# State-space mixer: softplus and products between input units, bounded differences on ScalarE, output tiles inside the head loop and the norm

## What is computed

```python
def pool_ssd_mixer(h, w_in, pool_w, pool_scale, conv_w, conv_b, dt_bias, a_log, d_skip, norm_g, w_out):
    proj = h @ w_in
    u_pool, z, xbc, dt_raw = jnp.split(proj, [...], axis=-1)
    y_pool = multiscale_pool(u_pool, pool_w, pool_scale)
    xbc = jax.nn.silu(causal_depthwise_conv(xbc, conv_w, conv_b))
    xs, bm, cm = jnp.split(xbc, [...], axis=-1)
    dt = jax.nn.softplus(dt_raw + dt_bias)
    a = -jnp.exp(a_log)
    y = ssd_chunked(xh, dt, a, bm, cm)           # two chunks of 128 tokens, 16 heads of 64, 2 groups, state 128
    y = (y + d_skip * xh).reshape(...) * jax.nn.silu(z)
    y = group_rmsnorm(y) * norm_g                # two groups of 512
    return jnp.concatenate([y_pool, y], axis=-1) @ w_out
```

## Time and profile before

| | us |
|---|---|
| median of three runs | 2388.79 |
| lowest, highest of them | 2385.91, 2414.0 |
| the profiled execution, its own time | 2413.47 |
| its span in the profile | 2411.6 |

### The profile page before, as it was taken

The page is one execution under the profiler, slowest core; times in us unless marked ns, Lnnn a source line. Parts: engine busy times, 40 slices in busy tenths (PEclk is TensorE's granted clock), DMA queues, the critical chain, the costliest instruction groups (busy, mean ns, idle before and its releaser), DMA issues.

```text
span 2411.6 us, 46117 instructions
## 1 busy us (share of the span) xinstructions
PE 2282.1 (95%) x18404; PEld 2192.5 (91%) x18404; DVE 1414.0 (59%) x2021; ACT 1166.9 (48%) x1559; POOL 496.2 (21%) x250
## 2 busy tenths in 40 slices
PE   8989999988999899998999999998999999789998
PEld 7869799987999899996899999996899999778998
DVE  4554289955689859685468653365633434356544
ACT  5411166546556544464344454455544443545654
POOL 0013000010000135421035434410044400000343
PEclk9869699999999899996899999998999999889999
DMA  6200167843388568752268845542355455513552
GB/s 247 101 4 1 36 249 301 314 160 122 132 322 298 193 244 331 277 214 96 75 228 349 297 175 191 187 169 105 129 195 195 147 191 195 149 70 123 192 176 103
DMA packets 62224, 439.06 MB, mean 182 GB/s; under 512 B 7228, under 2 KB 7612, under 8 KB 9638
## 3 DMA queue, kind: packets, MB, share of 16 engines
q1 hardware_dynamic: 59472, 430.75, 48.5%
q0 software_dynamic: 976, 2.63, 0.7%
q10 hardware_dynamic: 1670, 4.17, 0.5%
HBM read 434.89 MB, written 2.62 MB: 181 GB/s over the span
## 4 chain that ended last, share of the span: by engine, by line
PE 77%; DVE 10%; issue 6%; ACT 5%; DMA 2%; DVEq 1%; POOL 0%; SPq 0%; ACTq 0%; POOLq 0%
PE ps L276 19%; PE ps L278 19%; PE ps L277 19%; DVE mix L580 3%; PE ps L290 2%; PE ps L298 2%; PE ps L292 2%; PE ps L404 1%; ACT w_hi L255 1%; DVE w_lo L261 1%; PE ps L393 1%; DVE acc L688 1%; DMA ring<-in_weights 1%; DVE acc L682 1%; PE ps L953 1%
## 5 line engine op out<-in xcount | busy, mean ns | idle before, releaser
L276 PE MATMUL ps<-h_hi,w_hi 128*128 128x256 f32 x3512 | 985.1, 280 | 9.4 <-DVE h_lo L2180 4.9
L277 PE MATMUL ps<-h_lo,w_hi 128*128 128x256 f32 x3512 | 982.1, 280 | 0.0
L278 PE MATMUL ps<-h_hi,w_lo 128*128 128x256 f32 x3512 | 981.7, 280 | 0.0
L261 DVE TENSOR_TENSOR w_lo<-ring,w_hi 128x2048 fp32r<-128x2048 f32 x273 | 626.0, 2294 | 566.0 <-ACT w_hi L255 561.6
L255 ACT ACTIVATE w_hi<-ring 128x2048 fp32r<-128x2048 f32 x335 | 640.6, 1913 | 186.8 <-PE ps L278 175.3
L276 PEld LDWEIGHTS ps<-h_hi,w_hi 128*128 128x128 f32 x3512 | 665.6, 190 | 13.1 <-DVE h_lo L2180 5.1
L277 PEld LDWEIGHTS ps<-h_lo,w_hi 128*128 128x128 f32 x3512 | 668.8, 190 | 0.1
L278 PEld LDWEIGHTS ps<-h_hi,w_lo 128*128 128x128 f32 x3512 | 664.5, 189 | 0.0
L276 PE MATMUL ps<-g_hi,w_hi 128*128 (+1 forms) x1232 | 346.8, 282 | 12.5 <-DVE g_lo L710 12.0
L277 PE MATMUL ps<-g_lo,w_hi 128*128 (+1 forms) x1232 | 345.4, 280 | 0.0
L278 PE MATMUL ps<-g_hi,w_lo 128*128 (+1 forms) x1232 | 345.3, 280 | 0.0
(11 more groups left out here) (395 smaller groups left out, 2588.7 us busy)
## 6 DMA issues: line engine op xcount, KB each, us to landing
ring<-in_weights SPq DMA_DIRECT2D x335, 1024.0 KB, 4.8
mix<-in_modw SPq DMA_DIRECT2D x72, 1024.0 KB, 5.0
mix<-in_c_ssd ACTq DMA_DIRECT2D x1, 1536.0 KB, 8.1
bias_rows<-mix POOLq DMA_DIRECT2D x1, 1536.0 KB, 36.0
x<-in_x SPq DMA_DIRECT2D x1, 1024.0 KB, 4.9
mix<-in_c SPq DMA_DIRECT2D x2, 512.0 KB, 5.8
mix<-bias_rows POOLq DMA_DIRECT2D x1, 1024.0 KB, 8.2
out_xT<-hf SPq DMA_DIRECT2D x1, 1024.0 KB, 4.3
```

Of the source, the lines that this page charges most:

```text
L261: dve.tensor_tensor(w_lo[:, n % SLOTS], ring[:, n % SLOTS], w_hi[:, n % SLOTS], ALU.subtract).then_inc(lo_ready[n % SLOTS], 1)
L276: pe.matmul(o, w[0], a_hi, start=first, stop=False, **kw)
L277: pe.matmul(o, w[0], a_lo, start=False, stop=False, **kw)
L278: return pe.matmul(o, w[1], a_hi, start=False, stop=last, **kw)
```

## The change

The order of the weight columns becomes B and C, x, dt (padded to 128), u, z; so dt is in the seventh unit and the last half unit holds the end of z. The loop is written out for 13 units, and what used to stand after it is put between units: C B^T and the transposed B ahead of unit 6, the transposes of x and of dt and dt*a ahead of unit 10, the sums ahead of unit 11, the rows ahead of unit 12. The softplus runs in turn 7 and 8; ScalarE takes Silu of z straight from PSUM. The bounded difference moves from VectorE (`min(row - a_cs, 0)`) to ScalarE (`Relu(a_cs - row)`, and Exp of its negative). The y products alternate between the two heads. `warm` matmuls stand in the pair loop, and `fill` puts tiles of the first two ab_out units in the loop and in the norm. The squares of the first three quarters move from ScalarE to GpSimd, which also adds them in part. `hi` and `lo` of one unit, ab_in + 15 (the third unit of ab_out), are no longer issued in the loop: `hi` stands after the pair loop, `lo` behind the last `low`.

```diff
@@ pool
-            pool.wait_ge(z_free, zbase["ab_in"] + 8)
+            pool.wait_ge(z_free, zbase["ab_in"] + 9)
...
+            for j in range(3):
+                s = slice(2 * j, 2 * j + 2)
+                pool.wait_ge(*after(f"dve:ssd.yz{j}"))
+                pool.tensor_tensor(hf[:, s], sd_y[:, s], sd_y[:, s], ALU.mult).then_inc(*step(f"pool:ssd.gsq{j}"))
...
+        SD_Y_BANK = (5, 6, 7, 6)
+        SD_FILL = {5: 3, 6: 3, 7: 3, 8: 3}
@@ pe
-            a_stage_pe(pe, "ab_in", "ssd", 13, half_last=True)
+            for l in range(count["ab_in"]):
+                n = BASE["ab_in"] + l
+                if l == 6:
...
+                if l == 10:
+
+                    pe.wait_ge(*after("act:ssd.silu5"))
+                    pe.wait_ge(*after("dve:ssd.cbT"))
+                    pe.wait_ge(*after("act:ssd.btok"))
...
+                    pe.wait_ge(*after("dve:ssd.adt"))
...
+            def outer(p):
+                for e in range(2):
+                    done = pe.matmul(bank((p + 1) % 2, 2, T)[:, e], sd_sel[0:16, 2 * p + e],
+                                     sd_row[0:16].rearrange("p c t -> p (c t)"), start=True, stop=True)
+                done.then_inc(*step(f"pe:ssd.a{p}"))
...
+            queue = [(l, kk, b) for l in range(2) for kk in range(2) for b in range(8)]
...
+                    if kk == 0 and b == 0:
+                        pe.wait_ge(lo_ready[s], u // SLOTS + 1)
+                        if l == 0:
+                            pe.wait_ge(*after("dve:ssd.plo"))
+                            pe.wait_ge(*after("dve:ssd.y0"))
...
+            pe.wait_ge(*after("act:ssd.row"))
+            outer(0)
             pe.wait_ge(z_free, zbase["ab_in"] + 13)
...
+            outer(1)
+            pe.wait_ge(*after("dve:ssd.xdt"))
+            warm(3)
             pe.wait_ge(*after("dve:ssd.xdec"))
...
+            warm(2)
+            for p in range(1, 9):
+                if 2 <= p < 8:
+
+                    pe.wait_ge(*after(f"act:ssd.ea{p - 2}"))
+                    outer(p)
+                if p == 2:
...
+                if p < 5:
+                    warm(1)
+                else:
+                    fill(SD_FILL[p])
                 q = p - 1
...
+                pe.wait_ge(*after(f"dve:ssd.g{q}"))
+                o = [ps[SD_Y_BANK[q // 2]][64 * e:64 * e + 64, T * (q % 2):T * (q % 2) + T] for e in range(2)]
+                for e in range(2):
+                    pe.matmul(o[e][:, 0:P], sd_xdt[:, 0, 2 * q + e], sd_dm[q % 2][:, e, 0], start=True, stop=True)
...
+            fill(5)
+            pe.wait_ge(*after("pool:ssd.gs0"))
...
+            fill(2)
+            pe.wait_ge(*after("act:ssd.gsq3"))
...
+            fill(4)
             pe.wait_ge(*after("dve:ssd.rs"))
...
-            b_stage_pe(pe, "ab_out", ["dve:ssd.plo", None, "dve:ssd.ylo0", "dve:ssd.ylo1", "dve:ssd.ylo2", "dve:ssd.ylo3"], "ssd")
+            fill(len(queue))
+            for l in range(2, 6):
+                pe.wait_ge(*after(f"dve:ssd.ylo{l - 2}"))
@@ act
+            for p in range(8):
+                act.wait_ge(*after(f"pe:ssd.a{p}"))
+                if p >= 2:
+                    act.wait_ge(*after(f"pe:ssd.y{p - 2}"))
+                for e in range(2):
+                    for c in range(NCH):
+                        done = act.activation(sd_dm[p % 2][:, e, c], bank((p + 1) % 2, 2, NCH, P)[:, e, c], ACT.Relu, scale=-1.0,
+                                              bias=sd_acs[:, c, 2 * p + e:2 * p + e + 1])
+                done.then_inc(*step(f"act:ssd.m{p}"))
+                act.activation(sd_ce[p % 2], bank((p + 1) % 2, 2, NCH, P)[:, :, 1], ACT.Exp).then_inc(*step(f"act:ssd.ea{p}"))
+                act.wait_ge(*after(f"act:ssd.m{p}"))
+                act.activation(sd_dm[p % 2], sd_dm[p % 2], ACT.Exp, scale=-1.0).then_inc(*step(f"act:ssd.e{p}"))
...
+                if p == 3:
+
+                    act.wait_ge(*after("pe:ssd.pool"))
...
+            hi(act, BASE["ab_in"] + 12 + SLOTS)
@@ dve
+                if l < 12:
+                    lo(dve, BASE["ab_in"] + l + SLOTS)
...
+                if p == 4:
+                    dve.wait_ge(*after("act:ssd.phi"))
+                    for g in range(4):
+                        done = dve.scalar_tensor_tensor(out=h_lo[:, g], in0=bank(2 + g // 2, 2, T)[:, g % 2],
...
+            gated(0)
+            for j in range(1, 4):
+                gated(j)
+                low(j - 1)
+            low(3)
+            lo(dve, BASE["ab_in"] + 12 + SLOTS)
             b_stage_dve(dve, "ab_out", owed=2)
```

More of the change, by code:

```diff
@@ L1735, in ssd_pe @@
             pe.wait_ge(*after("dve:ssd.xdec"))
-            pe.wait_ge(*after("act:ssd.btok"))
-            pe.wait_ge(*after("act:ssd.dend"))
-            pe.wait_ge(*after("act:ssd.row"))
             for g in range(2):
@@ L1768, in ssd_pe @@
-            pe.wait_ge(*after("pool:ssd.d"))
-            for g in range(4):
-                done = pe.matmul(bank(6 + g // 2, 2, T)[:, g % 2], sd_pw[:, g], sd_pd[:, g], start=True, stop=True)
-            done.then_inc(*step("pe:ssd.pool"))
-            for j in range(4):
-                pe.wait_ge(*after(f"act:ssd.gsq{j}"))
-                for c in range(NCH):
-                    for b in (2 * j, 2 * j + 1):
-                        g = b // 4
-                        done = pe.matmul(ps[1][:, 2 * c + g:2 * c + g + 1], hf[:, b, c * P:(c + 1) * P], ones[:, 0:1],
-                                         start=b == 0 and c == 0, stop=b == 7 and c == 1, skip_group_check=True)
+                done.then_inc(*step(f"pe:ssd.prev{g}"))
@@ new lines, in ssd_pe @@
+            sums = ps[1]
+            fill(5)
+            pe.wait_ge(*after("pool:ssd.gs0"))
+            for c in range(NCH):
+                for b in range(2):
+                    pe.matmul(sums[:, 2 * c:2 * c + 1], hf[:, b, c * P:(c + 1) * P], ones[:, 0:1],
+                              start=b == 0 and c == 0, stop=b == 1 and c == 1, skip_group_check=True)
+            pe.wait_ge(*after("pool:ssd.gs1"))
+            for c in range(NCH):
+                pe.matmul(sums[:, 2 * c + 1:2 * c + 2], hf[:, 4, c * P:(c + 1) * P], ones[:, 0:1], start=False, stop=False,
+                          skip_group_check=True)
@@ L1780, in ssd_pe @@
+            fill(2)
+            pe.wait_ge(*after("act:ssd.gsq3"))
+            for c in range(NCH):
+                for b in (6, 7):
+                    done = pe.matmul(sums[:, 2 * c + 1:2 * c + 2], hf[:, b, c * P:(c + 1) * P], ones[:, 0:1],
+                                     start=False, stop=b == 7 and c == 1, skip_group_check=True)
             done.then_inc(*step("pe:ssd.gss"))
+            fill(4)
             pe.wait_ge(*after("dve:ssd.rs"))
@@ L1891, in ssd_dve @@
+            dve.wait_ge(*after("dve:ssd.xdt0"))
             dve.wait_ge(*after("act:ssd.dend"))
@@ L1923, in ssd_dve @@
[L1923 to L1928 removed]
+                    dve.wait_ge(*after("pool:ssd.d"))
+                    for r in (q - 1, q):
+                        done = dve.scalar_tensor_tensor(out=sd_y[:, r], in0=sd_cb[:, r], scalar=V("ssd_d_2", r),
+                                                        in1=bank(SD_Y_BANK[q // 2], 2, T)[:, r % 2], op0=ALU.mult, op1=ALU.add)
```

305 lines of the change are left out of this document (160 added, 145 removed).

## The result

The changed kernel takes 2382.94 us (median of 20 runs, 2359.61 to 2404.44) against 2395.69 of the kernel before measured with it (20 runs, 2385.91 to 2414.0). The ratio on record is 0.9913, 95% interval [0.9889, 0.9937]: 15 to 27 us less, and inside the 2% band. The quotient of the two medians is 0.9947, 12.8 us less, which lies outside that interval; so the gain in the whole time is known only roughly, and the stages of the profiles say more. The forecast was 2369.3, between 2357 and 2396, and 19.5 us less.

A forecast was written before the change was run, and what follows sets the result against it. TensorE carries 77% of the chain; the middle takes 67.1 us at mean clock 0.59. Terms 7.0, 31.5, 15.4, 21.8 and 1.6 make 77.3 against 101.3; less 4.5 for the clock, 19.5 us gained: 2369.3, range 2357 to 2396.

The forecast's parts named there:

- (a): Loop over the ab_in units: work moved in and waits added ahead of unit 10 make it 7.0 us longer.
- (b): End of unit 12 to y of pair 0, at full clock: 8.3 us.
- (c): Pairs 2 to 4, pool map and outer of pair 5: 10.1 us; four Relus on ScalarE take 1.25.
- rival D: Relu switches tables, or dt*a comes too late for the loop; some 19 us more, 2388; chance 0.06.
- (d): New wait ahead of the first fill, for the pool's h_lo: 13.5 us from y0's end, TensorE waits 3.4.
- (e): Pairs 5 to 8, with fills, y products and outers: 9.7 us with handoffs.
- the clock: Falls in the wait ahead of the first fill, back after about one and a half pairs: 4.5 us.
- Rivals A: Clock holds through all pairs: 24.0 us less, 2364.8; chance 0.23.
- B: Clock falls ahead of the first fill, stays down to the norm: 9 instead of 4.5 us, 2373.8; chance 0.20.
- Rival C: Clock falls at the two outers and the wait for dt*x, padding does not restore it: 3.9 slower, 2392.7; chance 0.09.
- (f): Norm 7.3 us, then a second new wait, for unit 15's late lo, TensorE idle 5.0: 15.4 in all.
- (g): Four ab_out units left after the wait: 21.8 us, plus 1.6 of slow start.

The follow-up runs named there:

- dt_early: Changed kernel with VectorE's short softplus operations ahead of the split of unit ab_in + 11; mixer 158.4 us, ratio 0.9917 to the kernel before.
- vector_bound: Changed kernel with the bounded differences back on VectorE, ScalarE keeping the two Exps; mixer 160.4 us, ratio 0.9907 to the kernel before.
- fill_late: Changed kernel with fills from pair 6 on, four each, and one warm matmul in pair 5; mixer 155.0 us, ratio 0.9897 to the kernel before.
- after: The changed kernel itself, first profiled execution; mixer 156.2 us, ratio 0.9913 to the kernel before.
- again: The changed kernel unaltered, run and profiled a second time; mixer 157.8 us, ratio 0.9923 to the kernel before.
- lo_early: Changed kernel with VectorE's split of the third ab_out unit moved ahead of the norm's root; mixer 153.8 us, ratio 0.9894 to the kernel before.
- tiles_after: Changed kernel without fills in loop or norm, one warm matmul per pair, all 32 tiles behind the norm; mixer 158.9 us, ratio 0.9910.
- head_order: Changed kernel with each pair's y products in the old order, first head, then second; mixer 165.4 us, ratio 0.9887 to the kernel before.
- no_warm: Changed kernel with its nine warm matmuls left out; mixer 156.9 us, ratio 0.9919 to the kernel before.
- joined: Changed kernel with early third-unit split, fills from pair 6, softplus ahead of the split, and early fourth-unit split; mixer 148.3 us, ratio 0.9872.
- joined_lean: The joined kernel without its ten warm matmuls; mixer 146.0 us, median 2367.46, ratio 0.9874 to the kernel before.
- softplus_after: Changed kernel with softplus, its transposes, sums, rows and dt*x back behind the last input unit; mixer 166.2 us, ratio 0.9947.

## Why the prediction was right, point by point

The forecast of 19.5 us less meets 19.2 and 17.6 in the two profiles and 15 to 27 in the ratio. The absolute 2369.3 was 13.6 low: 6.9 of that is the kernel before, whose median is 2395.69 over 20 runs and was 2388.79 over three. The rest is the 12.8 between the medians, where 19.5 was forecast. Part of the agreement is luck: the terms below were forecast as 7.0, 8.3, 13.5, 14.2, 15.4 and 23.4 us and measured as 7.5, 7.8, 13.0, 12.3, 17.0 and 24.2. They miss by up to 1.9 us, and the misses cancel to nothing. Another execution of the same kernel has 4.2 us more in one of them.

- (a) The loop: 7.0 forecast, 7.5 measured, with a wait of 2.14 for the 2.1 taken. It came by the way named, `lo` ahead of three short operations; one of them took 1.50, beside GpSimd, where it takes 0.41 in dt_early. The sum has no price for the clock here; it fell at this wait in four of the eight executions that have it. dt_early removes it, 2.2 us.
- (b) 8.3, measured 7.8 (1098.07 to 1105.9), at full clock.
- (c) Four Relus take 1.12 to 1.25 us, mostly 1.14 (1.25 taken), and no table load lies between Relu and Exp; rival D's first half falls, and with the 2.14 us of (a) its second. Where the Relus stand made no difference: vector_bound gives the same.
- (d) From the end of the first y to the first fill 13.0 us (13.5 forecast), of them 2.7 a wait (3.4), ended by L2015. Its length was right; but taking it out saved none of that length (fill_late).
- (e) and the clock: 9.7 and 4.5 forecast. (The 9.7 is the sum with two `outer`, for pairs 6 and 7; "three times" counts the one of pair 5, which is in (c).) Measured 12.3 in the first profile (1118.90 to 1131.2), so 2.6 for the clock, and 4.2 us more in the second, so 6.8. The step that failed is that I took one price. The same wait left 3.4, 13.7, 13.7 and 17.1 us at half clock between first and last y (after, again, lo_early, dt_early). Rivals A (0 us for the clock) and B (9) are not two worlds: the execution of after lies between A and the forecast in the pairs, that of again between the forecast and B, and dt_early, 17.1 us at half clock, near B. Rival C falls: y7 ends 33.1 us after unit 12, not 51.5. Its first half, a fall at the start, did come, in six of the eleven executions with the softplus in the loop (tiles_after, head_order, dt_early, no_warm, joined, joined_lean), but each time for 3.4 us, and the clock was back by the first y, without the pad too.
- (f) 15.4 forecast, 17.0 measured, of them 5.03 the wait for the late split (5.0 forecast). The norm up to the end of the spread took 8.5 for 7.3, with 3.4 us at half clock that I hadn't counted.
- (g) 23.4 forecast, 24.2 measured.

What was hidden: the fills were booked as a gain in (e) and the 5.0 us as a loss in (f), which the sum gets right; that the second eats most of the first, so that fills and no fills come out alike, took tiles_after to see. By the runs, half of the gain is the softplus between the units: 8.4 to 10 us, the wait and the clock that falls in it taken together (softplus_after). The other half lies mostly between last y and spread, 14.6 to 7.3 and 6.3. There the pool map and part of the squares left the norm, and ten single-column sums stand for sixteen; but 11 of the 14.6 us were at half clock and 2.2 or none are now, which could be up to 5.6 us of it. No run takes order and clock apart there; that half is read from milestones, and argued.

## What to carry to other kernels

Work that is pulled ahead of a wait brings its engine earlier to the next thing; look up when that one is ready (here a weight split that stood behind the last low part), or the gain turns into idle time there. A stretch at the lower clock isn't by itself time to be won: first ask whether another engine's chain sets the end, and what the filling itself costs, since filling the waits here took 41 us of half clock away and 1.4 us of time. Where a short wait sits among small matmuls, reckon with the time at half clock around it as a range, and compare single profiles by stage and with their time at half clock beside them.
